# A 64 by 64 triangular inverse taken in blocks of 32, its corner formed by TensorE between the slots of a gate pass

## The reference

```
proj = rms_norm(h, mix_pre_g) @ w_in        # last 4096 columns: the gates
rw_seg, q, k, v, gate_a, gate_b = split(proj)
for each time t (two directions, 16 heads, state S is 64 x 64):
    sa = -S kk_t
    S  = S * w_t + sa (kk_t * a_t)^T + v_t k_t^T
    out_t = S r_t
merged = sigmoid(gate_a) * (y_a @ w_branch_a) + sigmoid(gate_b) * (y_b @ w_branch_b)
```

## Time and profile before

| | |
|---|---|
| median of three runs | 2523.3 us |
| the profiled execution | 2523.74 us, of which the span of the profile is 2522.0 us |
| TensorE matmul busy | 2387.4 us, 95% |
| DVE, ACT, POOL busy | 56%, 42%, 5% |
| mean granted TensorE clock | 0.973 |
| gate pass | from 1103.4 us to 1326.5 us of the span |

### The profile page before, as it was taken

One profiled execution on the slowest core, in us unless ns is written; L12 is line 12 of the kernel. 1 busy time (PEld: TensorE's weight loads), 2 busy tenths in 40 slices (PEclk: granted clock), 3 DMA queues, 4 the chain that ended last, 5 costly groups with the idle time before them and its releaser, 6 DMA issues.

```text
span 2522.0 us, 31770 instructions
## 1 busy us (share of the span) xinstructions
PE 2387.4 (95%) x12011; PEld 1941.2 (77%) x12011; DVE 1411.9 (56%) x1672; ACT 1055.5 (42%) x1394; POOL 129.4 (5%) x179
## 2 busy tenths in 40 slices
PE   8999999999989999998788977799899999999997
PEld 6888888888878777786577845688788888888886
DVE  4545544444556549969964445465654454455454
ACT  5444434444446645543232224344544443444443
POOL 1000000000000012210001130000000000000000
PEclk9999999999999999999998977899999999999999
DMA  7666555655557555675481023266566655666554
GB/s 244 188 190 190 190 193 192 192 186 190 190 164 235 174 163 182 194 240 168 141 245 55 10 85 94 92 234 208 169 190 188 189 189 192 193 191 189 189 190 140
DMA packets 227193, 443.79 MB, mean 176 GB/s; under 512 B 22780, under 2 KB 25104, under 8 KB 225680
## 3 DMA queue, kind: packets, MB, share of 16 engines
q1 hardware_dynamic: 207872, 399.82, 49.8%
q0 software_dynamic: 9104, 37.71, 4.5%
q10 hardware_dynamic: 10112, 4.83, 0.7%
HBM read 423.42 MB, written 18.87 MB: 175 GB/s over the span
## 4 chain that ended last, share of the span: by engine, by line
PE 57%; issue 29%; DVE 10%; ACT 2%; DMA 1%; POOL 0%; ACTq 0%; DVEq 0%; SPq 0%; POOLq 0%
PE ps L1384 16%; PE ps L1385 16%; PE ps L1386 16%; DVE wlo L854 3%; DVE z L1133 2%; DVE zt L1128 2%; DMA raw<-in_w_in 1%; PE ps L1630 1%; PE ps L1589 1%; PE ps L1615 1%; PE ps L1605 1%; PE ps L1631 1%; PE ps L1646 1%; ACT whi L471 0%; PE ps L1590 0%
## 5 line engine op out<-in xcount | busy, mean ns | idle before, releaser
L854 DVE TENSOR_TENSOR wlo<-raw,whi 128x1024 fp32r<-128x1024 f32 (+1 forms) x760 | 929.8, 1228 | 889.1 <-ACT whi L471 886.7
L471 ACT ACTIVATE whi<-raw 128x1024 fp32r<-128x1024 f32 (+1 forms) x760 | 800.8, 1058 | 1067.0 <-PE ps L1386 974.6
L1384 PE MATMUL ps<-whi,uhi 128*128 128x512 f32 (+1 forms) x2208 | 877.3, 397 | 33.5 <-DVE wlo L854 31.1
L1385 PE MATMUL ps<-wlo,uhi 128*128 128x512 f32 (+1 forms) x2208 | 865.2, 392 | 0.0
L1386 PE MATMUL ps<-whi,ulo 128*128 128x512 f32 (+1 forms) x2208 | 865.2, 392 | 0.0
L1384 PEld LDWEIGHTS ps<-whi,uhi 128*128 128x128 f32 x2208 | 418.8, 190 | 136.1 <-DVE wlo L854 40.9
L1386 PEld LDWEIGHTS ps<-whi,ulo 128*128 128x128 f32 x2208 | 418.3, 189 | 87.6
L1385 PEld LDWEIGHTS ps<-wlo,uhi 128*128 128x128 f32 x2208 | 419.0, 190 | 82.8
L1384 PE MATMUL ps<-whi,hthi 128*128 128x512 f32 x704 | 274.2, 389 | 0.0
L1386 PE MATMUL ps<-whi,htlo 128*128 128x512 f32 x704 | 273.9, 389 | 0.0
L1385 PE MATMUL ps<-wlo,hthi 128*128 128x512 f32 x704 | 273.9, 389 | 0.0
(11 more groups left out here) (266 smaller groups left out, 1491.9 us busy)
## 6 DMA issues: line engine op xcount, KB each, us to landing
raw<-in_ffn_w_gu SPq DMA_DIRECT2D x352, 512.0 KB, 3.4
raw<-in_ffn_w_down SPq DMA_DIRECT2D x176, 512.0 KB, 3.6
raw<-in_w_in SPq DMA_DIRECT2D x160, 512.0 KB, 3.6
raw<-in_w_out SPq DMA_DIRECT2D x32, 512.0 KB, 4.0
raw<-in_w_branch_a SPq DMA_DIRECT2D x16, 512.0 KB, 4.9
raw<-in_w_branch_b SPq DMA_DIRECT2D x16, 512.0 KB, 3.7
gate_dram<-gst_g POOLq DMA_DIRECT2D x8, 512.0 KB, 4.4
gbuf<-gate_dram POOLq DMA_DIRECT2D x8, 512.0 KB, 3.9
```

The source lines that it names most:

```text
L471: nc.scalar.activation(whi[:, s, :, 0:p.width], raw[:, s, :, 0:p.width], ACT.Copy).then_inc(hi_ready, 1)
L854: V.tensor_tensor(wlo[:, s, :, 0:p.width], raw[:, s, :, 0:p.width], whi[:, s, :, 0:p.width].bitcast(F32), ALU.subtract).then_inc(lo_ready, 1)
L1384: mm(o, at, w_, start=(j == 0 and k == 0), stop=False)
L1385: mm(o, at, l_, start=False, stop=False)
```

## The change

DVE eliminates only inside the two 32 x 32 diagonal blocks of each case, both in the same instruction (`zd` is a view of both; for that `z` gets one row more, [128, 65, 64], so that the second block lies at a constant step from the first). That is 31 steps in place of 63, and 2s(31-s) elements an instruction. A last DVE instruction copies the first block transposed into `zt`. The steps are spread by their work over slots 8 to 30.

The upper right block of the inverse is Z1 N12 Z2. TensorE forms it in four groups of 16 (pair, direction, chunk) cases of both heads: `vz_products(g)` (32 matmuls of 32 x 32 by 32 columns) after slot 42 + 3g, `z12_products(g)` (32 more) after slot 44 + 3g. ACT copies each result out of PSUM banks 4 to 7 in two instructions of 32 partitions by 512. The transposed block goes through HBM (`z1t_dram`, 512 KB) into `z1t`, whose contiguous runs there are 32 elements, 128 bytes. `zs` is read back in four pieces of 512 KB (two DMAs each), which POOL's queue issues when TensorE has done 36, 39, 42 and 45 slots. TensorE's and ACT's walk over the gate pass, a loop in the code before, is written out. The recurrence waits for `z12_ready` in place of `zs_in`.

```diff
-        s_z, (z, zt, _, gst_g) = room(("z", [P, C, C]), ("zt", [P, 32 * 32]), ...
+        s_z, (z, zt, _, gst_g) = room(("z", [P, C + 1, C]), ("zt", [P, HC * HC]), ...
+        Z_FIRST, Z_LAST, ZS_AT, VZ_AT, Z12_AT, ZG_STEP = 8, 30, 36, 42, 44, 3
@@ ACT
+            def vz_out(g):
+                act.wait_ge(vz_mm, g + 1)
+                for h in range(2):
+                    r = slice(C * h + HC, C * (h + 1))
+                    last = nc.scalar.activation(vz[r, PER_ZG * g:PER_ZG * (g + 1), :],
+                                                ps[r, 4 + g % 2, :].rearrange("p (j t) -> p j t", t=HC), ACT.Copy)
+                last.then_inc(vz_ready, 1)
...
+            for k in range(GATE_SLOTS):
+                fill(1)
+                for g in range(ZG):
+                    if k == VZ_AT + ZG_STEP * g + RING:
+                        vz_out(g)
+                    if k == Z12_AT + ZG_STEP * g + RING:
+                        z12_out(g)
@@ DVE
+            STEP_WORK = [120 + 2 * s * (HC - 1 - s) for s in range(HC)]
+            def steps_by(k):
+                share = min(max(k - Z_FIRST, 0) / (Z_LAST - Z_FIRST), 1)
+                return next(i for i in range(HC + 1) if sum(STEP_WORK[:i]) >= share * sum(STEP_WORK) - 1)
...
+                elif n:
+                    prod = zt[:, 0:2 * s * n].rearrange("p (k c t) -> p k c t", k=2, c=s)
+                    rest = zd[:, :, 0:s, s + 1:HC]
+                    link(V.tensor_tensor(prod, zd[:, :, 0:s, s:s + 1].broadcast_to((P, 2, s, n)),
+                                         zd[:, :, s:s + 1, s + 1:HC].broadcast_to((P, 2, s, n)), ALU.mult))
+                    link(V.tensor_tensor(rest, rest, prod, ALU.add))
                 else:
+                    V.tensor_copy(zt[:, :].rearrange("p (t c) -> p t c", c=HC),
+                                  z[:, 0:HC, 0:HC].rearrange("p c t -> p t c")).then_inc(z_done, 1)
@@ TensorE
-            walk(pe, p_gate, from_u(p_gate, None))
-            pe.wait_ge(zs_in, 32)
+            def vz_products(g):
+                if g == 0:
+                    pe.wait_ge(n_st, NM)
+                    pe.wait_ge(z1t_in, 32)
+                pe.wait_ge(zs_in[g], 32)
+                if g >= 2:
+                    pe.wait_ge(vz_ready, g - 1)
+                for j in range(PER_ZG):
+                    for h in range(2):
+                        a_, b_, mc = slice(C * h, C * h + HC), slice(C * h + HC, C * (h + 1)), PER_ZG * g + j
+                        last = mm(ps[b_, 4 + g % 2, j * HC:(j + 1) * HC], zs[a_, mc, HC:C], z1t[a_, mc, :], start=True, stop=True)
+                last.then_inc(vz_mm, 1)
...   (z12_products(g): the same with vz[b_], zs[b_, mc, HC:C] into ps[a_, 6 + g % 2], after vz_ready)
+            for k in range(GATE_SLOTS):
+                fill(1)
+                for g in range(ZG):
+                    if k == VZ_AT + ZG_STEP * g:
+                        vz_products(g)
+                    if k == Z12_AT + ZG_STEP * g:
+                        z12_products(g)
+            pe.wait_ge(z12_ready, ZG)
@@ POOL's queue
-            store_gates(range(6))
+            store_gates(range(3))
             pool.wait_ge(z_done, 1)
             pool.dma_start(z_dram..., z...).then_inc(z_out, 16)
+            pool.dma_start(z1t_dram..., zt[:, :]).then_inc(z1t_out, 16)
+            store_gates([3])
+            pool.wait_ge(z1t_out, 16)
+            for h in range(2):
+                pool.dma_start(z1t[C * h:C * h + HC, :, :], z1t_dram[h].rearrange("m c s t -> s (m c) t")).then_inc(z1t_in, 16)
             pool.wait_ge(z_out, 16)
-            for h in range(2):
-                pool.dma_start(zs[C * h:C * (h + 1), :, :], z_dram[h]...).then_inc(zs_in, 16)
-            store_gates(range(6, 8))
+            for g in range(ZG):
+                pool.wait_ge(slots_used, p_gate.n0 + ZS_AT + ZG_STEP * g)
+                for h in range(2):
+                    pool.dma_start(zs[C * h:C * (h + 1), PER_ZG * g:PER_ZG * (g + 1), :], z_dram[h, ms]...).then_inc(zs_in[g], 16)
+                if g == 1:
+                    store_gates([4])
+            store_gates(range(5, 8))
```

More of the change, by code:

```diff
@@ L63 @@
 NC_ = T // C
+HC = C // 2
 NM = 2 * NPAIR
@@ L306, in layer @@
         bon_in, bon_mm, bon_st, bon_out, v1_in = (sem(n) for n in ("bon_in", "bon_mm", "bon_st", "bon_out", "v1_in"))
-        n_mm, n_st, z_in, z_done, z_out, zs_in = (sem(n) for n in ("n_mm", "n_st", "z_in", "z_done", "z_out", "zs_in"))
+        n_mm, n_st, z_in, z_done, z_out = (sem(n) for n in ("n_mm", "n_st", "z_in", "z_done", "z_out"))
         n_out = [sem("n_out0"), sem("n_out1")]
+        z1t_out, z1t_in, vz_mm, vz_ready, z12_mm, z12_ready = (
+            sem(n) for n in ("z1t_out", "z1t_in", "vz_mm", "vz_ready", "z12_mm", "z12_ready"))
+        ZG = 4
+        zs_in = [sem(f"zs_in{g}") for g in range(ZG)]
+        PER_ZG = NM * NC_ // ZG
+        GATE_SLOTS = p_gate.chunks * p_gate.slots
+        Z_FIRST, Z_LAST, ZS_AT, VZ_AT, Z12_AT, ZG_STEP = 8, 30, 36, 42, 44, 3
         vb_in = sem("vb_in")
@@ L708, in _, with z12_out @@
             fill(1)
[L711 to L713 removed]
+            def vz_out(g):
[5 more added lines that the diff above has]
+                last.then_inc(vz_ready, 1)
+            def z12_out(g):
+                act.wait_ge(z12_mm, g + 1)
+                for h in range(2):
+                    r = slice(C * h, C * h + HC)
+                    last = nc.scalar.activation(zs[r, PER_ZG * g:PER_ZG * (g + 1), HC:C],
+                                                ps[r, 6 + g % 2, :].rearrange("p (j t) -> p j t", t=HC), ACT.Copy)
+                last.then_inc(z12_ready, 1)
+            gate_out = to_stage(p_gate, gst_g, ACT.Sigmoid, 3)
+            fill = filler(in_steps(p_gate, split_hi(p_gate), each_chunk(p_gate, gate_out), [], skip=RING))
+            for k in range(GATE_SLOTS):
[5 more added lines that the diff above has]
+                        z12_out(g)
+            gate_out(p_gate.turns - 1, 1)
             ahead(p_ya)
[L717 removed]
+            for g in range(ZG):
+                act.wait_ge(zs_in[g], 32)
             for b in range(2):
@@ L1107, in _ @@
             fill(1)
[L1111 to L1116, removed]
+            ones = z[:, 0:C, :].rearrange("p c t -> p (c t)")[:, 0:C * C:C + 1]
+            zd = z[:, :, :].rearrange("p c t -> p (c t)").rearrange("p (k x) -> p k x", k=2)[:, :, 0:HC * C].rearrange(
+                "p k (c t) -> p k c t", t=C)[:, :, :, 0:HC]
+            STEP_WORK = [120 + 2 * s * (HC - 1 - s) for s in range(HC)]
+            def steps_by(k):
+                share = min(max(k - Z_FIRST, 0) / (Z_LAST - Z_FIRST), 1)
+                return next(i for i in range(HC + 1) if sum(STEP_WORK[:i]) >= share * sum(STEP_WORK) - 1)
             def step(s):
+                n = HC - 1 - s
                 if s == 0:
@@ L1138, in _ @@
                     split_lo(p_gate)(p_gate.n0 + k, 0, k // p_gate.slots, k % p_gate.slots)
-                for s in range(steps_before(k), steps_before(k + 1)):
+                for s in range(steps_by(k), steps_by(k + 1)):
                     step(s)
             ahead(p_ya)
-            dve.wait_ge(zs_in, 32)
+            for g in range(ZG):
+                dve.wait_ge(zs_in[g], 32)
             V.memset(sv[0:C, 0, 0, :], 0.0)
@@ L1568, in _, with z12_products @@
                     low_rank(m + 2)
-            walk(pe, p_gate, from_u(p_gate, None))
-            pe.wait_ge(zs_in, 32)
+            def vz_products(g):
[10 more added lines that the diff above has]
+                last.then_inc(vz_mm, 1)
+            def z12_products(g):
+                pe.wait_ge(vz_ready, g + 1)
+                if g >= 2:
+                    pe.wait_ge(z12_ready, g - 1)
+                for j in range(PER_ZG):
+                    for h in range(2):
+                        a_, b_, mc = slice(C * h, C * h + HC), slice(C * h + HC, C * (h + 1)), PER_ZG * g + j
+                        last = mm(ps[a_, 6 + g % 2, j * HC:(j + 1) * HC], vz[b_, mc, :], zs[b_, mc, HC:C], start=True, stop=True)
+                last.then_inc(z12_mm, 1)
+            fill = filler(in_steps(p_gate, from_u(p_gate, None), [], []))
+            for k in range(GATE_SLOTS):
+                fill(1)
+                for g in range(ZG):
+                    if k == VZ_AT + ZG_STEP * g:
[3 more added lines that the diff above has]
+            pe.wait_ge(z12_ready, ZG)
             for b in range(2):
```

32 lines of the change are left out of this document (15 added, 17 removed).

## The result

The changed kernel takes 2489.63 us at the median (2487.94 to 2489.90, 4 runs) beside 2523.44 (2521.17 to 2523.97) for the kernel before on the same chip: a ratio of 0.9865 [0.9849, 0.9880], 33.8 us less. Timed again on another chip it was 2490.96, ratio 0.9874 [0.9859, 0.9889]. The forecast was 2501 with a range from 2491 to 2515. The sign and the place were right; the gain is half as large again, and the time lies just under the range.

What follows compares the result with a forecast made beforehand. TensorE's queue bounds the kernel, with DVE bounding the gate pass's second window. 174.1 + 1.7 + 1.0 + 22.7 + 1.5 = 201.0 us replaces the pass's 223.1, 22.1 less, giving 2501 us, range 2491 to 2515.

Steps and rivals of the forecast that it cites:

- DMAs: Gate pass, slots 29 to 42: extra transfers mostly absorbed by the ring of weights, 1.5 us left, bounds 0 and 17.
- TensorE's products: Gate pass: eight groups of 64 records at 0.038 us plus 0.4, 2.8 us each, 22.7 in all, bounds 12 and 34.6.
- DVE's elimination: Gate pass, slots 8 to 29: steps fall from 111 to 32.0 us, so DVE just stops being the bound; 1.0 us put back.
- second window: Gate pass, 30 slots after the first 20: 38.2 us lost to DVE's chain of waits, expected to go.
- first window: Gate pass, first 20 slots: 56.1 us for 54.4, so 1.7 lost, expected to stay.
- third's 9.0: Gate pass, last 14 slots: 9.0 us lost to one event, zs read back and slot 63's weights late; expected to go.
- sign of a stall: Gate pass: a raw load of 12 us or more after slot 29 would show the forecast wrong.
- costs the clock: Rival, gate pass: the lower clock follows each group, 12.8 us more, 2514; chance 0.09.
- The stall of the ring: Rival, slots 29 to 36: DMAs meet and a late-load event returns, 7.0 us more, 2508, two 2516; chance 0.12.
- Tiles of 32: Rival, TensorE's groups: tiles of 32 don't overlap, a group 14.3 us, 92 more, 2593; chance 0.05.
- The two-block view: Rival, DVE's steps: the view of two blocks runs at half rate, 20.6 us more, with clock falls 2528; chance 0.03.
- the cheap product: Rival, TensorE's groups: products cost only 1.5 us a group, 2490; chance 0.09.

Runs made afterwards that it cites:

- e11: The changed kernel once more, unchanged, timed and profiled a second time beside the later versions: 2490.96 us.
- the probes: Two runs of the changed kernel with the four vz groups in other tile shapes and placements, z12 groups as control: 10.8 to 31.7 ns a record, control 17.6.
- the best version: Changed kernel with steps in slots 11 to 32, recurrence hand-over reordered, splits spread, and two groups' products sent in turn on four row groups: 2472.65 us, ratio 0.9803.
- e3: Kernel before with only DVE's part changed: two diagonal blocks eliminated, no corner formed, zs read back in one piece: 2478.06 us, ratio 0.9826.
- e6: Changed kernel with DVE's steps in slots 11 to 32 in place of 8 to 30: 2486.13 us, ratio 0.9855.
- e5: Changed kernel with all four pieces of zs issued at once when 36 slots are done: 2495.82 us, ratio 0.9892.
- e7: Changed kernel with DVE's 31 steps packed into slots 8 to 22 in place of 8 to 30: 2498.83 us, ratio 0.9910.
- e1: Changed kernel with its four vz groups in other shapes or one head after the other, corner not formed: 31.6, 30.9, 29.8 and 31.7 ns a record.
- e4: Changed kernel without TensorE's eight groups and ACT's sixteen copies, corner left out: 2481.25 us, ratio 0.9828.
- e8: Changed kernel with steps in slots 11 to 32 and the way from gate pass into recurrence reordered: 2478.77 us, ratio 0.9831.

## Why the prediction was off

| term, us | forecast | measured | from |
|---|---|---|---|
| 64 slots at full clock | 174.1 | 174.1 | 0.227 apart throughout |
| start of the pass, slot 9 | 1.7 | 4.3 | 0.2 in slot 0; one wait of 2.35 and the lower clock behind it |
| DVE's lag | 1.0 | 0 | no wait for `wlo` after slot 9 |
| eight groups | 22.7 | 10.9 | 8 x 1.36 |
| DMAs | 1.5 | 0 | no late weights in this profile; 4.3 in that of `e11` |
| not assigned | | 0.2 | the last matmul's own end |
| the pass | 201.0 | 189.5 | |

**The step that failed is TensorE's products.** The pass came out 11.5 us below the forecast, and this term alone is 11.8 us below its own. The other terms nearly cancel, which is luck: in the profile of `e11` slot 9 and the late weights together cost 7.0 us. The step took 38 ns a record from `n_products` because its tiles were the nearest in shape, and gave the lower price only 0.09. The row was no price of a record: the probes show that 16 records carry a fixed 0.14 us between them, and that the rest scales with the wider side of the tile, which the change halves. The 17.6 ns measured lie below the lower bound of 20, and entry and return cost 0.2 us outside the records, not 0.4. The forecast's sentence that half the columns can't be free was right and was not priced: halving 29.4 ns would have given 15 ns and a group of about 1.3 us. The stated range did not hold the forecast's own lower bounds either: with 12 us for the groups and 0 for the DMAs its sum gives 2489.

The Trainium skill's figure of some 60 cycles of overhead for each matmul ("TensorEngine Tiling (Array Packing)", Performance Considerations), which the forecast weighed as 25 ns, does not hold as a price of every record in the queue: 17.6 ns with two tiles in turn, 10.8 with four, 9.5 in the best version. For one tile it is not contradicted: its records come 31.6 ns apart, and with two tiles in turn, streaming 16 columns in place of 32 gained nothing. The warning of the same page of the Trainium skill (Restrictions and Gotchas) that row tiles can't use one bank at the same time did not show: both heads write one bank, and their records start 6 to 7 ns apart.

**DVE's elimination was right**, by instruction (0.65 us for 480 elements, forecast 0.69 with the gap behind it) and as a whole: DVE is busy 57.0 of the 59 us from 1128 to 1187, the stretch of its steps, and after slot 9 TensorE does not wait for it. What the forecast did not see is that the loss of 49 us was nearly all DVE's. `e3`, without products and with the old read, gains 44.7: the 38.2 of the second window, 1.5 of the first window's 1.7, and 5.0 of the third's 9.0, because DVE's steps had eaten the slack that the ring gives to a late load. The forecast removed all of that 9.0 and named the read for it; the sum was right, the cause half wrong.

**The first window got worse, not equal.** The forecast kept its 1.7 us, but 1.4 of them were no cost of the start: slot 20, at the window's end, came 1.26 us late behind DVE, and that went with DVE's steps. In their place comes the late slot 9. In the changed kernel three steps stand ahead of a split that TensorE needs, and they wait for `z` until 1127.2; `e6` shows it by moving them, a pass 3.2 us shorter.

**DMAs: right in kind, and not settled in size.** The forecast put 1.5 us on them, with bounds of 0 and 17. The same kernel shows 0 in one profile, where weights took 12.6 us at most and the ring held, and 4.3 us in the other, where they took up to 15.5. In the first, TensorE was 1.4 us later at slot 40, by its greater loss at slot 9, and the load for that slot landed 3.4 us faster. By the medians of `e5` the pieces are worth some 5 to 6 us. The forecast's sign of a stall, a load of 12 us or more, came up in both profiles, and TensorE waited for late weights in the second alone.

**The rivals.** No group costs the clock: it stays at 1.00 behind all eight. The stall of the ring did not come in the first profile; in that of `e11` it came, an event of 4.3 us in place of the rival's 8.5. Tiles of 32 overlap as those of 64 do, at half the price. The two-block view has the full rate. The one that came true is the cheap product, which named 1.5 us a group and 2490; measured were 1.36 and 2489.6.

## What to carry to other kernels

A row with few records is the price of a burst and not of a record: split off the fixed part, then scale by the dimension that changes, before you use it for a burst four times as long. When one engine bounds a stretch, the losses charged to transfers behind it may be its own, since it empties the buffers that would have covered them; ask what each later stall costs with full buffers. One profile without a late load does not show that there is none: here a second one of the same kernel had it. Independent small tiles should be sent in turn over as many row groups as there are.

## What was unexpected of the hardware

- A tile takes its next float32 record after about 1 ns a column of its wider side (32 or 64), whether it has 32 or 64 rows, and tiles in turn share that time. For 32 columns a record costs 31.7 ns with one tile, 17.6 with two, 10.8 to 9.5 with four, the edges of the burst included.
- The clock does not fall behind bursts of small tiles (eight of 1.13 us), nor behind eight waits of 0.3 to 1.0 us (`e7`). Around 2 us the length of the wait alone does not decide: the clock fell behind waits of 1.87 us (`e1`), 2.10 (`e3`) and 2.35 (slot 9), and it stayed up behind 1.85 (`e4`), 2.17 (slot 9 in `e11`) and 2.33 us (slot 41 of the kernel before). It fell behind the longer waits of 3.87 us (`e5`) and 6.64.
- A load of weights takes 15 to 16 us beside a read in runs of 256 bytes. What that cost was decided by how early it was issued: 8.7 us in the kernel before, 4.0 in `e3`.
- Open: why the load for slot 40 took 9.8 us in one execution of the changed kernel and 13.2 in another, and whether `e8`'s range (2477.25 to 2483.82) hides a second cause beside DVE's order.
